# Two prompt tiles and the samples as a dense pass over all experts; gathered V rows split 14 to 2

## The chip, the cores and the metric

One core of a Trainium2 chip. The time is that of one launch on the device, in microseconds; lower is better. Data is float32 throughout.

## What is computed

One decoder layer over 1024 prompt tokens and 64 sample tokens (8 sequences of 8), width 1024: a token mix (dilated window attention in three groups and a short gated convolution), then experts, then a last norm. The change is in the experts:

```python
def block(xb):                                   # per token, 8 heads
    q = (xb @ w_query).reshape(PEER_BLOCK, PEER_HEADS, 2, half)
    s1 = einsum('thd,kd->thk', q[:, :, 0], sub_keys[0]); s2 = ... q[:, :, 1], sub_keys[1]
    v1, i1 = top_k(s1, 16); v2, i2 = top_k(s2, 16)
    cand = v1[..., :, None] + v2[..., None, :]   # 256 sums
    top_s, top_pos = top_k(cand, 16)             # 16 of 128*128 experts
    gate = softmax(top_s)
    act = einsum('td,thkd->thk', xb, expert_u[eidx])
    return einsum('thk,thkd->td', gate * gelu(act), expert_v[eidx])
x = x + gate2 * out;  y = rmsnorm(x, norm_f_g)
```

`expert_u` and `expert_v` have 16384 rows of 1024 numbers (64 MB each). A token takes 128 rows of each.

## The kernel before, in words

Tokens lie in nine tiles of 128: 0 to 7 prompt, tile 8 (`PS`) the 64 samples. They go in four segments (`SEG_TILES`: tile 0; 1, 2; 3 to 5; 6, 7 and the samples). Two programs run beside each other on every engine.

The **background** is the token mix of a segment and then its queries: `chain_order` writes out the order of all uses of four PSUM banks (`psB`), keyed as `("qkv", g, z)`, `("conv", ...)`, `("s", ...)` (attention scores), `("mix", ...)`, `("out", ...)`, and at the end of a segment per tile and head `project`, `turn_q`, `score`. Every use is filled by TensorE and emptied by ScalarE (ACT) or VectorE (DVE); a bank can be filled again only when its use four places back is emptied. Weights come through three slots of `w`, loaded by SyncE (SP) in `weight_blocks` order. Each score (128 tokens x 256 numbers) is copied to memory by ACT.

The **jobs** are the experts: one job per tile and head, 72 in all (`JOBS`). For job s, DVE ranks the scores (`experts`, L1960 to L2022: 16 best of each half, 16 best of 256 sums, their numbers, the gates), GpSimd (POOL) gathers row k of `expert_u` for all 128 tokens by an indirect DMA into a ring (`gather_u`, L863) and of `expert_v` one job later (`gather_v`, L873), one row of each in turn. DVE forms the dot of each U row (`dot`, L2033, one fused instruction) and at the end of the job the coefficients (`coefs`, ends in L2073; waits once for ACT). The V rows are added up in two ways (`on_vector`): on DVE by multiply-add into `acc` (`add_row`, L2049), or on TensorE (`weigh`, L1251) by a matmul with a diagonal matrix that ACT writes (L1649) into the accumulators `psA`. Before, 8 of 16 rows went to either in the first 56 jobs and 5 to DVE, 11 to TensorE after. The sample tile has 64 tokens, so its 16 rows are gathered as 8 (`width`), two halves that TensorE folds at the end. After 8 jobs a tile is summed, gated, normed and stored (`gather_up`, `final`, `finish`).

What ties the two together is `limit(s, f)`: at fraction f of job s each engine runs its background up to the same key. The key is found by planned costs (`chain_cost`, a unit about 1 us of matmul) spread evenly between marks, and every engine meets the keys in its own fixed order:

```python
marks = [(0, lead)]
marks += [(HEADS * T0[g] - 3, number["score", item_of(HEADS * T0[g])]) for g in range(1, SEGS_N)]
marks += [(HEADS * T0[SEGS_N - 1] + 3, last_bg)]
```

So before, the marks are at jobs 0, 5, 21, 45 and 51, and by these costs a job has 62, 33, 28 and 16 units of background in turn; jobs 51 to 72 have none.

## Time and profile before

| | us |
|---|---|
| median of 3 runs | 4099.45 (4091.34 to 4104.18) |
| the profiled execution | 4089.54 |
| its span, first to last instruction | 4087.7 |
| TensorE busy (PE) | 3203.6, 78% |
| VectorE busy (DVE) | 2904.9, 71% |
| GpSimd busy (POOL) | 2238.6, 55% |
| ScalarE busy (ACT) | 671.2, 16% |
| mean granted TensorE clock | 0.875 of full |

"Busy" is the time with an instruction of that engine running, its waits left out. A float32 matmul shows as two halves, so counts of PE are twice those of the code; a transpose shows as one. The DMA share is the mean over 16 DMA engines and can pass 1.0, since packets overlap.

### The profile page before, as it was taken

To read this page: it belongs to the slowest core of one execution; us is meant where nothing else is said; L and a number is where in the kernel's file an instruction comes from. 1 tells how busy PE (TensorE), PEld (TensorE's weight loads), DVE (VectorE), ACT (ScalarE), POOL (GpSimd) and SP (SyncE) were. 2 spreads that over 40 slices of the span, in tenths; PEclk is the share of its full clock that TensorE was granted. 3 is DMA by queue.
4 is the path that set the end of the run, shared out by engine and by line. 5 is a ranking of instruction groups with operands and counts; after the bars stand their busy time and mean duration, and the time that the engine had idled before them with its cause. 6 is when DMAs were issued, how large, how long until landed. Compare 5 with 4: busy or idle time off the path is not lost.

```text
span 4087.7 us, 35782 instructions
## 1 busy us (share of the span) xinstructions
PE 3203.6 (78%) x10406; PEld 1817.5 (44%) x10406; DVE 2904.9 (71%) x6586; ACT 671.2 (16%) x1872; POOL 2238.6 (55%) x2189
## 2 busy tenths in 40 slices
PE   5987989888889998887888977677877765566566
PEld 2575757654445544554444543334544431122222
DVE  1215645678876687677887777767778888888887
ACT  0012021221012211222101331111111110010111
POOL 0003323555554566565665566545657677777765
PEclk8988979999997899998998888788988877788878
DMA  6989969999997899999999899999999999999998
GB/s 207 274 268 334 316 219 315 368 404 383 389 364 244 289 385 398 377 394 382 391 394 366 307 359 366 359 365 363 400 355 406 407 407 409 409 399 409 409 368 319
DMA packets 670924, 1458.83 MB, mean 357 GB/s; under 512 B 53745, under 2 KB 378737, under 8 KB 670705
## 3 DMA queue, kind: packets, MB, share of 16 engines
q0 software_dynamic: 313648, 1142.49, 72.4%
q1 hardware_dynamic: 316596, 267.84, 21.0%
q10 hardware_dynamic: 40488, 46.22, 3.3%
q8 instruction: 87, 1.43, 0.1%
q14 instruction: 105, 0.86, 0.1%
HBM read 1422.53 MB, written 33.83 MB: 356 GB/s over the span
## 4 chain that ended last, share of the span: by engine, by line
DMA 17%; DVE 9%; POOL 9%; PE 8%; issue 5%; SPq 3%; ACT 1%; ACTq 0%; DVEq 0%; POOLq 0%
DMA peer_vring<-in_expert_v,peer_idx 12%; POOL peer_uring L863 4%; POOL peer_vring L873 4%; PE peer_psA L1251 4%; DVE peer_uring L2033 3%; DMA peer_uring<-in_expert_u,peer_idx 2%; DVE peer_acc L2049 2%; SPq L715 2%; SPq L711 1%; DMA peer_w<-in_w_in 1%; DMA peer_w<-in_w_attn_o 1%; PE peer_psB L1075 1%; PE peer_psB L1098 1%; PE peer_psB L1143 1%; DMA peer_arena<-in_x_prompt 1%
## 5 line engine op out<-in xcount | busy, mean ns | idle before, releaser
L1251 PE MATMUL peer_psA<-peer_vring,peer_diag 128*128 128x512 f32 x2336 | 1321.4, 704 | 527.2 <-DMA peer_vring<-in_expert_v,peer_idx 345.9
L873 POOL DMA_INDIRECT peer_vring<-in_expert_v,peer_idx x1088 | 1115.9, 1026 | 1129.2 <-PE peer_psA L1251 837.1
L2033 DVE CUSTOM_DVE_ANT_0 peer_uring<-peer_uring,peer_psH 128x1024 f32<-128x1024 f32 x1088 | 1320.8, 1214 | 327.3 <-DMA peer_uring<-in_expert_u,peer_idx 322.5
L863 POOL DMA_INDIRECT peer_uring<-in_expert_u,peer_idx x1088 | 1117.0, 1027 | 498.9 <-issue 299.2
L1251 PEld LDWEIGHTS peer_psA<-peer_vring,peer_diag 128*128 128x128 f32 x2336 | 485.6, 222 | 1184.5 <-issue 999.5
L2049 DVE SCALAR_TENSOR_TENSOR peer_acc<-peer_vring,peer_coef,peer_acc 128x1024 f32<-128x1024 f32 x495 | 637.1, 1287 | 89.8 <-DMA peer_vring<-in_expert_v,peer_idx 84.3
L1143 PE MATMUL peer_psB<-peer_hT,peer_w 128*128 128x128 f32 (+3 forms) x1152 | 277.0, 399 | 32.7 <-DMA peer_w<-in_w_in 32.5
L1220 PE MATMUL peer_psB<-peer_w,peer_hT 128*128 128x256 f32 x1152 | 275.8, 395 | 30.0 <-DMA peer_w<-in_w_query 29.3
L1036 PE MATMUL peer_psB<-peer_w,peer_hT 128*128 128x384 f32 (+1 forms) x864 | 294.9, 496 | 1.4 <-issue 0.7
L1164 PE MATMUL peer_psB<-peer_hT,peer_w 128*128 128x128 f32 (+3 forms) x1024 | 257.8, 407 | 35.0 <-DMA peer_w<-in_w_attn_o 35.0
L1220 PEld LDWEIGHTS peer_psB<-peer_w,peer_hT 128*128 128x128 f32 x1152 | 229.2, 201 | 89.3 <-DMA peer_w<-in_w_query 31.5
L1143 PEld LDWEIGHTS peer_psB<-peer_hT,peer_w 128*128 128x128 f32 x1152 | 199.2, 193 | 116.7 <-DMA peer_w<-in_w_in 36.3
L1164 PEld LDWEIGHTS peer_psB<-peer_hT,peer_w 128*128 128x128 f32 x1024 | 182.7, 198 | 111.6 <-DMA peer_w<-in_w_attn_o 39.5
L1036 PEld LDWEIGHTS peer_psB<-peer_w,peer_hT 128*128 128x128 f32 (+1 forms) x864 | 161.8, 190 | 131.3 <-issue 44.1
L1698 ACT ACTIVATE peer_g<-peer_g 128x16 f32<-128x16 f32 (+1 forms) x72 | 15.5, 215 | 1139.5 <-DVE peer_g L2063 1138.0
L1649 ACT ACTIVATE peer_diag<-peer_ident,peer_coef 128x128 f32<-128x128 f32 x584 | 178.3, 387 | 54.9 <-DVE peer_coef L2073 54.9
L1832 DVE TENSOR_REDUCE peer_mx<-peer_psB 128x1 f32<-128x512 f32 (+2 forms) x92 | 56.1, 626 | 124.0 <-PE peer_psB L1075 123.4
L1193 PE MATMUL peer_psB<-peer_w,peer_mT 128*128 128x384 f32 (+3 forms) x432 | 130.3, 458 | 6.3 <-issue 4.5
L1075 PE MATMUL peer_psB<-peer_w,peer_mT 64*128 64x256 f32 (+3 forms) x272 | 121.6, 532 | 0.0
L1098 PE MATMUL peer_psB<-peer_w,peer_arena 128*128 128x64 f32 x648 | 102.0, 317 | 24.2 <-ACT peer_arena L1511 24.0
L1098 PEld LDWEIGHTS peer_psB<-peer_w,peer_arena 128*128 128x128 f32 x648 | 99.1, 235 | 35.9 <-issue 35.9
L1193 PEld LDWEIGHTS peer_psB<-peer_w,peer_mT 128*128 128x128 f32 (+1 forms) x432 | 80.8, 188 | 59.0 <-issue 19.7
(201 smaller groups left out, 2738.0 us busy)
## 6 DMA issues: line engine op xcount, KB each, us to landing
peer_w<-in_w_in SPq DMA_DIRECT2D x136, 512.0 KB, 9.0
peer_w<-in_w_in SPq DMA_DIRECT2D x24, 1536.0 KB, 17.1
peer_w<-in_w_query SPq DMA_DIRECT2D x32, 1024.0 KB, 17.0
peer_w<-in_w_ada SPq DMA_DIRECT2D x16, 1536.0 KB, 8.0
peer_uring<-in_expert_u,peer_idx POOLq DMA_INDIRECT x1088, 11.4
peer_vring<-in_expert_v,peer_idx POOLq DMA_INDIRECT x1088, 11.2
peer_w<-in_w_conv_o SPq DMA_DIRECT2D x32, 384.0 KB, 10.0
peer_w<-in_w_o SPq DMA_DIRECT2D x8, 1536.0 KB, 22.2
```

The lines of the kernel that those rows point to most:

```text
L863: pool.indirect_dma_start(out=uring[:, r % U, :], out_offset=None, in_=io["expert_u"], in_offset=bass.IndirectOffsetOnAxis(ap=idx[:, s % 4 ...
L873: pool.indirect_dma_start(out=vring[:, r % V, :], out_offset=None, in_=io["expert_v"], in_offset=bass.IndirectOffsetOnAxis(ap=idx[:, s % 4 ...
L1036: last = pe.matmul(dst[0:R, 0:WQKV], hT[:, k, i * P:i * P + R], wv[:, k, :], start=(k == 0), stop=(k == DC - 1))
L1098: last = pe.matmul(bank(key_o)[:, 0:HD], pT[:, t_slot[g, it, b] % 2, (at % 4) * P:(at % 4 + 1) * P], vv[:, kb, col:col + HD], start=(at == ...
L1143: last = pe.matmul(dst[:, 0:m], wv[:, k, part, :], hT[:, k, 0:m], start=(k == 0), stop=(k == DC - 1))
L1164: last = pe.matmul(dst[:, 0:m], wv[:, KC_AT[q] + k, :], src[:, k, 0:m], start=(k == 0), stop=(k == KC[q] - 1))
L1193: last = pe.matmul(dst[0:R, 0:e - a], mT[:, k, i * P:i * P + R], wv[:, k, :], start=(k == 0), stop=(k == DC - 1))
L1220: last = pe.matmul(dst[:, 0:KD], hT[:, k, j * P:(j + 1) * P], wv[:, k, :], start=(k == 0), stop=(k == DC - 1))
L1251: last = pe.matmul(psA[:, c * 512:(c + 1) * 512], diag[:, a % DG, :], vring[:, r % V, c * 512:(c + 1) * 512], start=first, stop=False, ski ...
L1649: act.activation(diag[:, a % DG, :], ident[:], ACT.Copy, scale=coef[:, s % 4, k:k + 1]).then_inc(diag_set, 1)
L2033: dve.tensor_tensor_reduce(uring[:, r % U, :], uring[:, r % U, :], psH[:], 1.0, 0.0, ALU.mult, ALU.add, act_[:, k:k + 1]).then_inc(u_used, 1)
L2049: dve.scalar_tensor_tensor(out=acc[:], in0=vring[:, r % V, :], scalar=c, in1=acc[:], op0=ALU.mult, op1=ALU.add).then_inc(v_added, 1)
```

## The change

- Jobs are only those of tiles 0 to 5 (`TD = 6`, 48 jobs). In them `on_vector` gives 14 of 16 V rows to DVE, all but k = 5 and 11. The U ring has 8 rows, not 9. The half-wide jobs go.
- A table in memory has a number for each of 16384 experts and each of the 320 tokens of tiles 6, 7 and samples (21 MB). POOL zeroes it by 8 DMAs, one after each of jobs 0 to 7.
- The 24 scores of segment 3 are not stored. DVE ranks each straight from its bank, as part of the background (`rank`), ACT forms its exponentials (`raise_gates`), and POOL adds the 16 gates per token to the table by 16 indirect DMAs (`scatter`), each of one number per partition. A scatter waits for the one of the previous head of its tile.
- Behind the last score the background has the dense pass (`dense_order`), 128 blocks of 128 experts: SP loads the block of U and the table's rows, and of V three blocks later; TensorE turns U (`ut`, 8 transposes), forms all dots for 320 tokens (`at`, 8 matmuls of 320 columns); ACT squares, DVE and ACT form the gelu, DVE multiplies by the table's gates; TensorE multiplies by V (`vd`, for four blocks at a time, three tiles and two halves), and DVE adds that to sums in memory on the chip. SP reads the table only when all scatters have landed, and asks for the second block of U behind that.
- The marks of `limit` are at jobs 0, 5, 21 and 48. By the planned costs jobs 21 to 48 have 92 units each.
- At the end the three tiles are gated, normed and stored.

```diff
 PS = SEQ // P
 SEG_TILES = ((0,), (1, 2), (3, 4, 5), (6, 7, 8))
+TD = 6
...
-JOBS = NT * HEADS
-WINDOW = 56
+JOBS = TD * HEADS
+ND = NT - TD
+DENSE_AT = tuple(d * P for d in range(ND))
+TDN = (ND - 1) * P + NS
+N_EXP = KEYS * KEYS
+CHUNKS = N_EXP // P
+GROUP = 4
+V_LAG = 6
...
 def on_vector(s, k):
-    return k in ((1, 3, 5, 7, 9, 11, 13, 15) if s < WINDOW else (2, 5, 8, 11, 14))
+    return k not in (5, 11)
...
+def dense_order():
+
+    order = [("ht", d, c) for d in range(ND) for c in range(2)]
+    for c in range(CHUNKS + V_LAG):
+        if c < CHUNKS:
+            order += [("ut", c, half) for half in range(2)]
+        group, d = divmod(c - V_LAG, GROUP)
+        if group >= 0 and d < ND:
+            order += [("vd", group, d, half) for half in range(2)]
+        if 1 <= c <= CHUNKS:
+            order += [("at", c - 1)]
+    return order
...
-        marks += [(HEADS * T0[g] - 3, number["score", item_of(HEADS * T0[g])]) for g in range(1, SEGS_N)]
-        marks += [(HEADS * T0[SEGS_N - 1] + 3, last_bg)]
+        marks += [(HEADS * T0[g] - 3, number["score", item_of(HEADS * T0[g])]) for g in range(1, SEGS_N) if T0[g] < TD]
+        marks += [(JOBS, last_bg)]
...
+            def scatter(n):
+                t, it = dense_items[n]
+                g, R = place(t)[0], rows_of(t)
+                yield min(number["score", it] + 24, number["ht", 0, 0])
+                if n == 0:
+                    pool.wait_ge(zeroed, 16 * 8)
+                old = n - sum(t2 >= TD for t2 in SEG_TILES[g])
+                if old >= dense_before(g):
+                    pool.wait_ge(scattered[old % 4], 16 * TOPK * (old // 4 + 1))
+                pool.wait_ge(d_ready, n + 1)
+                for k in range(TOPK):
+                    pool.indirect_dma_start(
+                        out=io["table"], out_offset=bass.IndirectOffsetOnAxis(ap=d_idx[0:R, n % 4, k:k + 1], axis=0),
+                        in_=d_gate[0:R, n % 4, k:k + 1], in_offset=None, compute_op=ALU.add).then_inc(scattered[n % 4], 16)
...
+            for c in range(CHUNKS + 3):
+                if c < CHUNKS:
+                    if c >= 3:
+                        wait_filled(sp, ("ut", c - 3, 1))
+                    elif c:
+                        sp.wait_ge(zeroed, 16 * 8)
+                    sp.dma_start(u_slot[c % 3], io["expert_u"][c * P:(c + 1) * P, :]).then_inc(eu_in[c % 3], 16)
+                    if c == 0:
+                        for r in range(4):
+                            sp.wait_ge(scattered[r], 16 * TOPK * (len(dense_items) // 4))
+                        for r in range(2):
+                            wait_emptied(sp, ("st", 4 * r + 3))
+                    if c >= 4:
+                        sp.wait_ge(ct_set, c - 3)
+                    sp.dma_start(g_slot[c % 4], table[c * P:(c + 1) * P, :]).then_inc(g_in[c % 4], 16)
...
+                    elif key[0] == "at":
+                        for k in range(DC):
+                            last = pe.matmul(dst[:, 0:TDN], UT[:, c % 2, k * P:(k + 1) * P], HT[:, k, :],
+                                             start=(k == 0), stop=(k == DC - 1))
+                    else:
+                        group, d, half = key[1:]
...
+                            last = pe.matmul(dst[0:R, :], COEF[:, c % (2 * GROUP), at:at + R],
+                                             v_slot[c % (2 * GROUP)][:, 512 * half:512 * (half + 1)],
+                                             start=(c % GROUP == 0), stop=(c % GROUP == GROUP - 1))
...
+                    dve.scalar_tensor_tensor(out=t2, in0=t2, scalar=1.0, in1=a, op0=ALU.add, op1=ALU.mult).then_inc(a_inner, 1)
+                    dve.wait_ge(g_in[c % 4], 16 * (c // 4 + 1))
+                    dve.tensor_tensor(g2, a, g2, ALU.mult).then_inc(out_of(key), 1)
...
+                dve.tensor_tensor(a, a, g_slot[c % 4], ALU.mult).then_inc(ct_set, 1)
```

The order on POOL in jobs 28 and 29, where before only U and V gathers took turns. L954 and L964 are the gathers of U and V, L979 the scatters; the sixteen of one head are one row.

```order
L954 DMA peer_uring<-in_expert_u,peer_idx 128x1024
L964 DMA peer_vring<-in_expert_v,peer_idx 128x1024
L979 DMA gates_of_experts<-peer_d_gate,peer_d_idx 5242880x1 x16
L954 DMA peer_uring<-in_expert_u,peer_idx 128x1024
L964 DMA peer_vring<-in_expert_v,peer_idx 128x1024
L979 DMA gates_of_experts<-peer_d_gate,peer_d_idx 5242880x1 x16
L954 DMA peer_uring<-in_expert_u,peer_idx 128x1024
L964 DMA peer_vring<-in_expert_v,peer_idx 128x1024
```

So from U row 12 of job 28 on, 16 or 32 scatters stand behind each pair of gathers, for eleven pairs; the last 160 stand in one piece behind row 7 of job 29.

The order on DVE in the same jobs, where before a ranking was cut into 15 pieces over a job's 16 rows. L2353 is the dot, L2369 the addition, L1983 to L2034 a ranking of the new kind (this is its start).

```order
L2353 ISA peer_uring,peer_act<-peer_uring,peer_psH 128x1024
L2353 ISA peer_act 128x1
L2369 SCALAR_TENSOR_TENSOR peer_acc<-peer_vring,peer_coef,peer_acc 128x1024
L1983 MAX peer_mT<-peer_psB 128x8 x2
L1986 MAX_INDEX peer_d_i<-peer_mT,peer_psB 128x8
L1987 MATCH_REPLACE peer_mT<-peer_mT,peer_psB 128x128
L1986 MAX_INDEX peer_d_i<-peer_mT,peer_psB 128x8
```

24 whole rankings stand from row 6 of job 28 to row 7 of job 29, one or two behind each row. TensorE in the dense pass reads as below; L1070 is `at`, L1060 `ut`, L1078 `vd`, L1410 a weighed row.

```order
L1070 MATMUL peer_psB<-peer_arena,peer_mT 128x320 x8
L1060 MATMUL peer_psB<-peer_ident,peer_w 128x128 x8
L1078 MATMUL peer_psB<-peer_w,peer_arena 128x512 x4
L1410 MATMUL peer_psA<-peer_vring,peer_diag 128x512 x2
L1078 MATMUL peer_psB<-peer_w,peer_arena 128x512 x4
L1070 MATMUL peer_psB<-peer_arena,peer_mT 128x320 x8
L1060 MATMUL peer_psB<-peer_ident,peer_more 128x128 x8
```

Two weighed rows stand in some seven blocks of this, where before 8 or 11 stood in each job.

## Rows read from the trace of the kernel before

**Rows 1.** The page: all packets, and those of the plain queue.
```profile
DMA packets 670924, 1458.83 MB, mean 357 GB/s; under 512 B 53745, under 2 KB 378737, under 8 KB 670705
...
q1 hardware_dynamic: 316596, 267.84, 21.0%
```

**Rows 2.** Table of stretches: PE, PEld, DVE, ACT, POOL busy, clock, DMA share, GB/s.
```profile
400.00:820.00 420.00, 384.32 (x1509) 276.14 (x1508) 240.76 (x561) 79.55 (x214) 162.26 (x162) 0.92 0.88 307
820.00:1150.00 330.00, 288.53 (x885) 162.87 (x884) 263.89 (x581) 47.57 (x127) 192.22 (x188) 0.93 1.04 390
1150.00:1420.00 270.00, 240.84 (x850) 137.74 (x849) 186.99 (x434) 71.59 (x206) 131.59 (x130) 0.82 0.80 288
1420.00:1700.00 280.00, 246.17 (x722) 139.61 (x721) 216.69 (x459) 47.91 (x105) 166.06 (x160) 0.95 1.03 385
1700.00:3240.00 1540.00, 1200.11 (x3964) 686.87 (x3962) 1175.77 (x2597) 278.28 (x793) 938.20 (x901) 0.87 1.01 374
...
3290.00:3910.00 620.00, 372.53 (x621) 135.40 (x619) 524.36 (x1186) 58.29 (x198) 467.51 (x467) 0.81 1.02 404
```

**Rows 3.** The same stretches for L2073 alone, one instruction per job, on DVE.
```profile
400.00:820.00 420.00, 1.04 (x6) 0.92 0.88 307
...
1700.00:3240.00 1540.00, 4.90 (x28) 0.87 1.01 374
...
3290.00:3910.00 620.00, 2.62 (x15) 0.81 1.02 404
3910.00:4087.00 177.00, 1.16 (x7) 0.83 0.90 346
```

**Rows 4.** The same table for L1251 alone, the weighed rows on PE.
```profile
1700.00:3240.00 1540.00, 500.95 (x894) 184.11 (x892) 0.87 1.01 374
```

**Rows 5.** The groups by line: weighed rows, dots, additions.
```profile
L1251 PE MATMUL peer_psA<-peer_vring,peer_diag 128*128 128x512 f32 x2336 | 1321.4, 704 | 527.2 <-DMA peer_vring<-in_expert_v,peer_idx 345.9
...
L2033 DVE CUSTOM_DVE_ANT_0 peer_uring<-peer_uring,peer_psH 128x1024 f32<-128x1024 f32 x1088 | 1320.8, 1214 | 327.3 <-DMA peer_uring<-in_expert_u,peer_idx 322.5
...
L2049 DVE SCALAR_TENSOR_TENSOR peer_acc<-peer_vring,peer_coef,peer_acc 128x1024 f32<-128x1024 f32 x495 | 637.1, 1287 | 89.8 <-DMA peer_vring<-in_expert_v,peer_idx 84.3
```

**Rows 6.** Timeline of PE: start, duration (us); x counts halves or transposes.
```profile
405.06 0.49 PE L1047 MATMUL peer_psB<-peer_ident,peer_arena 128*128 128x128 f32 x3
405.39 1.88 PE L1251 MATMUL peer_psA<-peer_vring,peer_diag 128*128 128x512 f32 x4
...
1018.53 5.32 PE L1036 MATMUL peer_psB<-peer_w,peer_hT 128*128 128x384 f32 x16
1023.69 3.60 PE L1251 MATMUL peer_psA<-peer_vring,peer_diag 128*128 128x512 f32 x8
1027.13 5.32 PE L1036 MATMUL peer_psB<-peer_w,peer_hT 128*128 128x384 f32 x16
```

**Rows 7.** The table for PE alone: busy, clock, DMA share, GB/s.
```profile
1000.00:1060.00 60.00, 59.79 (x173) 1.00 1.01 374
...
1200.00:1300.00 100.00, 86.06 (x322) 0.73 0.71 257
```

**Rows 8.** Groups by line and form: DVE and ACT reading PSUM.
```profile
L1511 ACT ACTIVATE peer_arena<-peer_psB 128x512 f32<-128x512 f32 x68 | 38.6, 590 | 56.2 <-PE peer_psB L1111 55.6
...
L1769 DVE TENSOR_TENSOR peer_arena<-peer_psB,peer_arena 128x512 f32<-128x512 f32 x16 | 11.0, 689 | 7.1 <-PE peer_psB L960 6.9
...
L1769 DVE TENSOR_TENSOR peer_arena<-peer_psB,peer_arena 128x320 f32<-128x320 f32 x8 | 3.9, 485 | 0.0
```

**Rows 9.** Groups by line: three of the instructions of a ranking.
```profile
L1993 DVE TENSOR_TENSOR peer_eq<-peer_ab,peer_iota 128x512 f32<-128x512 uint32 x72 | 49.7, 690 | 0.2
...
L1963 DVE FIND_INDEX8 peer_i<-peer_v,peer_sc 128x8 uint32<-128x128 f32 x144 | 41.4, 288 | 0.0
...
L1974 DVE MAX8 peer_best<-peer_eq 128x8 f32<-128x256 f32 x72 | 30.4, 422 | 0.5
```

**Rows 10.** The timeline of POOL in the pure gathering stretch.
```profile
3521.32 0.94 POOL L873 DMA_INDIRECT peer_vring<-in_expert_v,peer_idx  x1 [0.30 <-issue]
```

More of the change, by code:

```diff
@@ L123, in constants @@
         "rope": rope, "pmask": pmask, "smask": smask, "ident": np.eye(P, dtype=np.float32),
+        "columns": np.array([[DENSE_AT[d] + min(p, rows_of(TD + d) - 1) for d in range(ND)] for p in range(P)], np.float32),
         "iota": np.tile(np.arange(TOPK, dtype=np.float32), (P, 1)),
@@ L270, in added_by @@
     for s in range(JOBS):
-        for k in range(width(s)):
+        for k in range(TOPK):
             mine = on_dve if on_vector(s, k) else on_pe
@@ L875, in gather_v, with background @@
                     in_offset=bass.IndirectOffsetOnAxis(ap=idx[:, s % 4, k:k + 1], axis=0)).then_inc(v_in[r % V], 16)
+            def scatter(n):
[8 more added lines that the diff above has]
+                pool.wait_ge(d_ready, n + 1)
+                for k in range(TOPK):
+                    pool.indirect_dma_start(
+                        out=io["table"], out_offset=bass.IndirectOffsetOnAxis(ap=d_idx[0:R, n % 4, k:k + 1], axis=0),
+                        in_=d_gate[0:R, n % 4, k:k + 1], in_offset=None, compute_op=ALU.add).then_inc(scattered[n % 4], 16)
+            def background():
+                for n in range(len(dense_items)):
+                    yield from scatter(n)
+            pace = Pace(background())
+            wide = io["table"].rearrange("(p q m) o -> p q (m o)", p=P, m=512)
+            pool.memset(zero, 0.0).then_inc(zero_set, 1)
+            pool.wait_ge(zero_set, 1)
             for s in range(JOBS + 1):
@@ L1272, in _ @@
                     weigh(r)
-                    pace.up_to(limit(s, min(0.9, (i + 3) / len(rows))))
-            pe.wait_ge(summed, NT)
-            for c in range(2):
-                for i in range(2):
-                    last = pe.matmul(psA[0:NS, c * 512:(c + 1) * 512], ident[:, i * NS:(i + 1) * NS],
-                                     acc[:, c * 512:(c + 1) * 512], start=(i == 0), stop=(i == 1))
-            last.then_inc(folded, 1)
+                    pace.up_to(limit(s, min(0.9, (r % TOPK + 6) / TOPK)))
         @block.scalar
@@ L1600, in keep_queries @@
                         act.dma_start(io["scores"][(T0[g] + j) * HEADS + h],
-                                      sc_out[:, it % 2, :]).then_inc(sc_stored[it % 2], 16)
+                                      sc_out[:, q % 2, :]).then_inc(sc_stored[q % 2], 16)
+                    if i >= 3 and first + i - 3 in dense_no:
+                        yield from raise_gates(first + i - 3)
+                if first + count - 1 in dense_no:
+                    yield from raise_gates(first + count - 1)
@@ L1642, in spread @@
                 act.wait_ge(coef_set, s + 1)
-                for k in range(width(s)):
+                for k in range(TOPK):
                     r = rows_before(s) + k
@@ L1738, in background @@
                     yield from shift_tile(g, size(g) - 1)
+                    first, count = T0[g] * HEADS, size(g) * HEADS
+                    norms = {norm_at(g + 1, i): i for i in range(size(g + 1))} if g + 1 < SEGS_N else {}
+                    for i in range(count):
+                        if first + i in dense_no:
+                            yield from rank(first + i, dense_before(g))
+                        if i in norms:
+                            yield from norm_shift(g + 1, norms[i])
@@ new lines, in background, with raised @@
+                    if first + count - 1 in dense_no:
+                        yield number["score", first + count - 1]
+                        raised(dense_no[first + count - 1])
+                yield from weigh_all()
+            def raised(q):
+                dve.wait_ge(d_exp, q + 1)
+                if q:
+                    dve.wait_ge(d_ready, q)
+                link(dve.reciprocal(d_rg, d_dg[:, q % 2:q % 2 + 1]))
+                link.wait()
+                dve.tensor_scalar(d_gate[:, q % 4, :], d_eg[:, q % 2, :], d_rg, None, ALU.mult).then_inc(d_ready, 1)
@@ L2137, in _ @@
                     gather_up(t - 1)
-            finish(NT - 1)
+            finish(TD - 1)
+            dve.wait_ge(gate_s_in, 16)
+            for d in range(ND):
+                R = rows_of(TD + d)
+                for half in range(2):
+                    wait_emptied(dve, ("vd", CHUNKS // GROUP - 1, d, half))
+                gate_d = gate_s if TD + d == PS else gate2
+                dve.tensor_tensor(sums[d][0:R, :], sums[d][0:R, :], gate_d[0:R, :], ALU.mult).then_inc(d_gated, 1)
+                dve.wait_ge(d_gated, d + 1)
+                dve.wait_ge(xd_in[d], 16)
+                dve.tensor_tensor(xd[d][0:R, :], sums[d][0:R, :], xd[d][0:R, :], ALU.add).then_inc(d_x2, 1)
+            for d in range(ND):
+                R = rows_of(TD + d)
+                dve.wait_ge(d_rooted, d + 1)
+                link(dve.reciprocal(fin[0:R, 2, d:d + 1], fin[0:R, 1, d:d + 1]))
+                link.wait()
+                dve.scalar_tensor_tensor(out=xd[d][0:R, :], in0=xd[d][0:R, :], scalar=fin[0:R, 2, d:d + 1],
+                                         in1=gainf[0:R, :], op0=ALU.mult, op1=ALU.mult).then_inc(d_y, 1)
 def layer(nc, io):
```

359 lines of the change are left out of this document (287 added, 72 removed).

## The prediction

> **What bounds the kernel now.** I read the page first, then a table of stretches, then single lines. The page's totals [rows 1] say that 1459 MB move at a mean of 357 GB/s. The table of stretches [rows 2] says where that is the limit: from 820 to 1150, 1420 to 1700 and 3290 to 3910 us the DMA share is above 1.0, while TensorE (PE) and VectorE (DVE) have slack; 1700 to 3240 stands at 1.01. Two stretches are different. In 400 to 820 and 1150 to 1420 the share is 0.88 and 0.80 and PE is busy for 91% and 89% (384.32 of 420, 240.84 of 270): the dense layers and the attention of a segment set the pace there. The last step of a job's coefficients is one instruction per job, so its count [rows 3] dates the jobs: 6 end in 400 to 820, 28 in 1700 to 3240, 15 in 3290 to 3910, 7 after that; with one more in the 50 us between, 15 are left for 820 to 1700, and job 21 starts near 1700. A job of pure gathering costs 620/15 = 41.3 us: 32 rows of 512 KB (16.8 MB) at 404 GB/s. **So the last 850 us are bound by bytes, and the change removes bytes.** The question is what stands in their place.
>
> **What it takes off.** 24 jobs go, 8 of them half wide: 320 of 1088 rows of U and as many of V, 336 MB, 830 us at 404 GB/s. PE loses 488 of 584 weighed rows: four halves of a matmul each at 0.43 us (a run of 8 takes 3.44 us from start to start [rows 6]), 1.72 us a row, 840 us of work at full clock. DVE loses 320 dots at 1.21 us and gains 672 - 504 = 168 additions at 1.29 us [rows 5]: 388 us less, 216 more.
>
> **What it adds.** U and V once (134 MB), the table written and read (42 MB), 384 scatters of one number per partition, 24 rankings on DVE that were there before, and the dense pass. By the order that the program has now, this does not lie evenly: the background between jobs 21 and 48 is dealt out by planned cost, 92 units a job where it was 28. I cut the run into five parts.
>
> **A, up to job 21 (1700 us before).** The background is the same, jobs have 14 additions on DVE and 2 on PE. A pure job keeps DVE busy for 524.36/15 = 35.0 us; with 9 more additions 46.5 us. In the byte-bound stretches (11 jobs, 610 us) DVE was busy for 44 us of 55 a job; with 6 more additions it is at 52. That fits, with less to hide a late row in: +30 us. In the two other stretches (10 jobs) 6 rows of PE go (10.3 us a job) and 7.7 us of DVE come; these phases alternate between the engines, so I take them as -10 us together, between -90 (all PE's gain) and +60. Zeroing moves 21 MB, 52 us of transfers in jobs 0 to 7, half beside idle queues: +25. A = 1745, between 1640 and 1800.
>
> **B, job 21 to the first dense ranking (7.4 jobs).** PE without weighed rows was busy 1200.11 - 500.95 = 699 us in 1700 to 3240 [rows 2, 4] and 21 us in the 50 us after: 720 us for the rest of segment 2 and all of segment 3, spread over 30 jobs under the gathers. Of it the last 24 queries (16 halves of 256 columns and little else, 4.5 us each, 109 us) belong to C. 611 us and 15 rows at 1.72 are 637 us, now in 7.4 jobs. The nearest rows are the two stretches with PE at 91% and 89%, which would give 700 to 715; with 14 additions DVE answers attention later, so I take 740, between 650 (98% busy) and 850 (75%).
>
> **C, rankings and scatters (1.1 jobs).** 24 rankings follow each other on DVE. One is three passes over 512 numbers, ten instructions over 128, six over 256 [rows 9], and some 16 small ones of 0.1 to 0.2 us: 2.05 + 2.85 + 2.5 + 2.0 = 9.4 us, 226 us for all; before they were spread over 24 jobs. With 1.1 jobs of row work (51) DVE needs 277 us. POOL needs more: an indirect DMA takes it 0.94 us and 0.30 before it, 1.25 us [rows 10]. 16 items of 128 rows are 320 us, 8 items of 64 rows between 80 and 160 (I take 100), and 22 gathers between them 28. The first scatter waits for two rankings (25 us), and behind the last SyncE reads the table, which the first block needs (some 17 us with both landings). 490 us; PE has 110 us of work in it, and no dot can run ahead of the gathers behind the scatters. Below: 300, if an issue of 4-byte elements takes half as long and DVE sets the end. Above: no row shows a transfer that adds in memory. 40,960 elements, read and written, at the 43 ns that a packet of the plain queue cost (21.0% of 16 engines' 4088 us over 316596 packets [rows 1]) are 220 us on 16 engines, hidden; if an issue costs double because memory is both read and written, the part is 910. The Trainium skill (DMA: Bandwidth & Descriptors, "Anatomy of one DMA") fits a software-issued DMA at about 2.0 us plus its bytes; if these 512-byte scatters went singly at that, an estimate from that page, the sum would be some 290 us higher. The row stands among gathers whose transfers overlap, so the sum keeps 1.25.
>
> **D, the dense pass (18.5 jobs, 128 blocks).** Per block PE does 8 transposes at 0.11 us (three in 0.33), 16 halves of 320 columns at 5.16/16 x 320/384 = 0.269 us, and a quarter of 48 halves of 512 columns at 0.43 [rows 6]: 0.88 + 4.30 + 5.16 = 10.34 us, 1323 us in all, and 37 weighed rows make 1387. DVE: 18.5 x 46.5 = 860 us and per block three passes of 320 and 1.5 of 512 at 0.485 and 0.689 [rows 8], 319 us: 1179, and some 0.6 us per block of waiting for ScalarE's square, 1256. ScalarE: two copies of 512 at 0.59 [rows 8] and two shorter passes, about 2 us a block, hidden. Bytes: 310 + 134 + 21 MB at 404 GB/s, 1151 us, hidden. PE sets the end with DVE close behind and four PSUM banks between them, and ScalarE stands still at each job's end until the coefficients are out. I take PE at 88%, 1580 us, between 1420 (98%) and 1850 (75%).
>
> **E, the end**: last sums, three tiles of gate, norm and store: 25 us.
>
> **Sum**: 1745 + 740 + 490 + 1580 + 25 = 4580 us of span against 4087.7; 2 us lie around it, and the median of the runs is 10 us above the profiled one, so 4590. PE has replaced the transfers as the limit, and C is a hole in which nearly everything stands.
>
> **Rivals.**
> *Tight packing, 4150 (slower side or even).* A 1690, B 650, C 350, D 1430, E 25. For it: PE at 99.7% for 60 us at full clock [rows 7] with gathers beside it. Against: C needs cheap scatters.
> *Bytes stay the limit, 3920 (the other side).* -830 for gathers, +332 for U and V, +110 for the table and small loads, +220 for the scattered elements is about -170 against 4088. It decides if C hides behind gathers and PE never falls under 95%; PE's total, 3204 - 488 x 2.26 [rows 5] + 1323 = 3424 us, allows it, the order of C speaks against.
> *Half clock in the dense pass, 4850.* The granted clock was 1.00 where PE was 99.7% busy and 0.73 (a mix of 2.4 and 1.2 GHz) where it was 86% busy with short gaps [rows 7]. Gaps at every hand-over with DVE would stretch D from 1580 to some 1850. The Trainium skill (TensorE: Matmul & The Clock Gate, Part 1) has it that activity releases the throttle and idleness brings it back; by that rule it feeds itself.
> *Scatters dearer than gathers, 5000 and more.* C at 910 or above; no row speaks for it, none against.
>
> **Numbers.** Forecast 0.60, tight packing 0.14, bytes 0.07, half clock 0.13, slow scatters 0.06. All bounds at one end would give 4035 or 5435; taken as independent (root of the squares of 105, 90, 190, 160 below and 55, 110, 420, 270 above) they give 4306 and 5094, and the upper ends of C and D are rivals of their own, so the forecast alone stands for 4300 to 4850. The range goes to 4180 and 4900, for most of the tight case and of the half clock. 0.3% is about what a measurement of this kernel can tell from no change: faster 0.07, same 0.02, slower 0.91.
>
> **What would show it.** DMA share under 0.8 in the second half; PE idle and clock low in one stretch of 350 to 550 us near 2500, with POOL's scatters end to end and DVE on rankings first, then idle; jobs of 80 to 90 us in the dense pass with PE near 88%; jobs of about 100 us between 1745 and 2500. A dense pass with jobs under 77 us, or scatters issued in under 0.7 us, proves parts D or C wrong; gathers at 400 GB/s after 1745 would prove the whole reading wrong.

## The result, and the profile after

The changed kernel takes 4933.44 us (median of 4 runs, 4930.31 to 4947.73) against 4097.19 us for the kernel before on the same chip: 1.2047 times as long, 95% interval 1.2016 to 1.2078. The forecast was 4590 in a range up to 4900: the direction came out, the size did not. The profiled execution spans 4931.9 us (4087.7 before).

The page first: all packets and the two data queues, which answer to [rows 1], and the slices of PE and of the bandwidth.

```profile
PE   6978886567787699986785203105999999899995
...
PEclk9989798788668899858897656557999999999998
DMA  7899899999789998739973322227988989889984
...
DMA packets 679528, 1293.21 MB, mean 262 GB/s; under 512 B 96241, under 2 KB 431473, under 8 KB 679281
...
q0 software_dynamic: 273840, 828.06, 48.7%
q1 hardware_dynamic: 372324, 424.10, 26.6%
```

The bytes went down by 166 MB and the mean rate from 357 to 262 GB/s: after 1755 us, as the table below shows, transfers no longer set the pace. In PE's row there is a hole of some six slices (of 123 us each), in which the DMA digit is 2 or 3, and then an almost solid row of nines.

The table of stretches of the changed kernel, cut at the bounds of the parts A to E (PE, PEld, DVE, ACT, POOL busy, granted clock, DMA share, GB/s). It answers to [rows 2].

```profile
400.00:1755.00 1355.00, 1013.32 (x3458) 663.96 (x3466) 1037.55 (x2144) 207.98 (x520) 729.86 (x648) 0.80 0.95 344
1755.00:2600.00 845.00, 729.78 (x2766) 470.98 (x2773) 449.08 (x935) 163.34 (x455) 275.22 (x234) 0.84 0.79 256
2600.00:3375.00 775.00, 151.98 (x571) 122.16 (x571) 253.15 (x944) 32.49 (x114) 616.01 (x414) 0.59 0.28 30
3375.00:4890.00 1515.00, 1428.43 (x4752) 794.03 (x4752) 1102.93 (x2166) 308.94 (x653) 745.27 (x601) 0.98 0.87 314
4890.00:4932.00 42.00, 1.72 (x3) 0.25 (x1) 20.92 (x21) 7.06 (x13) 0.00 (x0) 0.54 0.30 100
```

And the same stretches for L2393, the last step of a job's coefficients, one instruction per job on DVE, as in [rows 3]:

```profile
400.00:1755.00 1355.00, 3.67 (x21) 0.80 0.95 344
1755.00:2600.00 845.00, 1.22 (x7) 0.84 0.79 256
2600.00:3375.00 775.00, 0.17 (x1) 0.59 0.28 30
3375.00:4890.00 1515.00, 3.31 (x19) 0.98 0.87 314
```

The jobs lie as the prediction put them: 21, then 7, one, and 19. The cuts are rounded: the first ranking starts at 2611.9 us and the first transpose of the dense pass at 3374.1, so by the events themselves B is some 12 us longer and C as much shorter. Set beside its sum:

| part | predicted (range) | measured | difference |
|---|---|---|---|
| A, to job 21 | 1745 (1640 to 1800) | 1755 | +10 |
| B, to the first dense ranking | 740 (650 to 850) | 845 | +105 |
| C, rankings and scatters | 490 (300 to 910) | 775 | +285 |
| D, dense pass | 1580 (1420 to 1850) | 1515 | -65 |
| E, end | 25 | 42 | +17 |
| span | 4580 | 4932 | +352 |

Each part is inside its own bounds, but two of them missed upwards together. The most is in C, where POOL is busy for 616 of 775 us, DVE for 253 and PE for 152. Below are the shares of the chain that ended last, the page's group of the scatters, and the instruction of a ranking in which DVE waits for them:

```profile
PE peer_psB L1078 14%; POOL gates_of_experts L979 11%; PE peer_psB L1070 10%; PE peer_psB L1323 3%; PE peer_psA L1410 3%; PE peer_psB L1302 2%; PE peer_psB L1234 2%; PE peer_psB L1257 2%; PE peer_psB L1060 2%; PE peer_psB L1195 2%; DVE peer_acc L2369 2%; DMA peer_vring<-in_expert_v,peer_idx 1%; DVE peer_uring L2353 1%; PE peer_psB L1379 1%; PE peer_psB L1352 1%
...
L979 POOL DMA_INDIRECT gates_of_experts<-peer_d_gate,peer_d_idx x384 | 587.2, 1529 | 176.8 <-issue 116.0
...
L2034 DVE TENSOR_SCALAR peer_d_idx<-peer_mT,peer_columns 128x16 uint32<-128x16 f32 x24 | 6.2, 260 | 333.8 <-DMA gates_of_experts<-peer_d_gate,peer_d_idx 333.5
```

POOL's timeline in the hole (start, duration in us, idle time before it in brackets). The last row is a scatter of 64 rows, of the sample tile; the others work on 128:

```profile
2757.96 1.56 POOL L979 DMA_INDIRECT gates_of_experts<-peer_d_gate,peer_d_idx  x1 [0.30 <-issue]
2759.82 0.99 POOL L954 DMA_INDIRECT peer_uring<-in_expert_u,peer_idx  x1 [0.30 <-issue]
2761.12 0.97 POOL L964 DMA_INDIRECT peer_vring<-in_expert_v,peer_idx  x1 [0.30 <-issue]
2762.40 1.61 POOL L979 DMA_INDIRECT gates_of_experts<-peer_d_gate,peer_d_idx  x1 [0.30 <-issue]
...
2794.32 1.41 POOL L979 DMA_INDIRECT gates_of_experts<-peer_d_gate,peer_d_idx  x1 [0.30 <-issue]
```

A gather is issued in 0.97 to 0.99 us (0.94 in [rows 10]). A scatter that adds takes 1.56 us, and hardly less with half the rows. It moves 512 bytes where a gather moves 512 KB. The detail of the scatters' line (duration in ns, first and last start, forms; then the time from issue to landing):

```profile
L979 POOL DMA_INDIRECT gates_of_experts<-peer_d_gate,peer_d_idx x384: 1404/1556/2408, 2633.2 to 3364.0; - x192
...
DMA to landing us min/median/max: 2.7/3.0/8.5
```

384 scatters are 587.2 us of POOL and 116.0 us between them, 703 us of the 733 from first to last. DVE stood still for 333.5 us in the rankings, because the scatters of the ranking four places back had not all landed and its indices could not yet be overwritten. A scatter has landed 3.0 us after its issue and the DMA share is 0.28, which speaks against a queue in the transfers; the runs below test it.

### The profile page after: what moved, and what is told of

Same layout as the page of the kernel before. It is cut to its first block, busy times and chain, and to the rows that moved or that the text cites. A ratio compares the mean times of both kernels' runs of the same rounds, so it can differ in the third digit from the quotient of the medians.

```text
span 4931.9 us, 42120 instructions
## 1 busy us (share of the span) xinstructions
PE 3644.5 (74%) x13062; PEld 2260.1 (46%) x13078; DVE 2970.1 (60%) x6503; ACT 769.5 (16%) x1870; POOL 2403.9 (49%) x1942
## 4 chain that ended last, share of the span: by engine, by line
PE 46%; POOL 13%; DVE 6%; DMA 5%; issue 5%; ACT 2%; SPq 1%; ACTq 0%; DVEq 0%; POOLq 0%
PE peer_psB L1078 14%; POOL gates_of_experts L979 11%; PE peer_psB L1070 10%; PE peer_psB L1323 3%; PE peer_psA L1410 3%; PE peer_psB L1302 2%; PE peer_psB L1234 2%; PE peer_psB L1257 2%; PE peer_psB L1060 2%; PE peer_psB L1195 2%; DVE peer_acc L2369 2%; DMA peer_vring<-in_expert_v,peer_idx 1%; DVE peer_uring L2353 1%; PE peer_psB L1379 1%; PE peer_psB L1352 1%
## 5 line engine op out<-in xcount | busy, mean ns | idle before, releaser
L954 POOL DMA_INDIRECT peer_uring<-in_expert_u,peer_idx x768 | 1037.1, 1350 | 1635.4 <-DVE peer_act L2353 1370.1
L2353 DVE CUSTOM_DVE_ANT_0 peer_uring<-peer_uring,peer_psH 128x1024 f32<-128x1024 f32 x768 | 925.5, 1207 | 119.2 <-DMA peer_uring<-in_expert_u,peer_idx 117.6
L964 POOL DMA_INDIRECT peer_vring<-in_expert_v,peer_idx x768 | 765.2, 996 | 471.2 <-issue 229.9
L2369 DVE SCALAR_TENSOR_TENSOR peer_acc<-peer_vring,peer_coef,peer_acc 128x1024 f32<-128x1024 f32 x666 | 851.6, 1279 | 8.1 <-DMA peer_vring<-in_expert_v,peer_idx 6.7
L1078 PE MATMUL peer_psB<-peer_w,peer_arena 128*128 128x512 f32 (+1 forms) x1536 | 692.1, 603 | 58.5 <-issue 57.7
L979 POOL DMA_INDIRECT gates_of_experts<-peer_d_gate,peer_d_idx x384 | 587.2, 1529 | 176.8 <-issue 116.0
L1070 PE MATMUL peer_psB<-peer_arena,peer_mT 128*128 128x320 f32 x2048 | 578.4, 436 | 0.0
L1070 PEld LDWEIGHTS peer_psB<-peer_arena,peer_mT 128*128 128x128 f32 x2048 | 386.9, 191 | 199.7 <-issue 58.7
L1078 PEld LDWEIGHTS peer_psB<-peer_w,peer_arena 128*128 128x128 f32 (+1 forms) x1536 | 261.6, 175 | 428.4 <-issue 425.0
L1410 PE MATMUL peer_psA<-peer_vring,peer_diag 128*128 128x512 f32 x384 | 225.9, 719 | 298.8 <-DMA peer_vring<-in_expert_v,peer_idx 235.3
L1410 PEld LDWEIGHTS peer_psA<-peer_vring,peer_diag 128*128 128x128 f32 x384 | 80.6, 225 | 385.8 <-issue 343.9
L2034 DVE TENSOR_SCALAR peer_d_idx<-peer_mT,peer_columns 128x16 uint32<-128x16 f32 x24 | 6.2, 260 | 333.8 <-DMA gates_of_experts<-peer_d_gate,peer_d_idx 333.5
```

What stands on the lines that cost most here:

```text
L954: pool.indirect_dma_start(out=uring[:, r % U, :], out_offset=None, in_=io["expert_u"], in_offset=bass.IndirectOffsetOnAxis(ap=idx[:, s % 4 ...
L964: pool.indirect_dma_start(out=vring[:, r % V, :], out_offset=None, in_=io["expert_v"], in_offset=bass.IndirectOffsetOnAxis(ap=idx[:, s % 4 ...
L979: pool.indirect_dma_start(out=io["table"], out_offset=bass.IndirectOffsetOnAxis(ap=d_idx[0:R, n % 4, k:k + 1], axis=0), in_=d_gate[0:R, n ...
L1070: last = pe.matmul(dst[:, 0:TDN], UT[:, c % 2, k * P:(k + 1) * P], HT[:, k, :], start=(k == 0), stop=(k == DC - 1))
L1078: last = pe.matmul(dst[0:R, :], COEF[:, c % (2 * GROUP), at:at + R], v_slot[c % (2 * GROUP)][:, 512 * half:512 * (half + 1)], start=(c % G ...
L1410: last = pe.matmul(psA[:, c * 512:(c + 1) * 512], diag[:, a % DG, :], vring[:, r % V, c * 512:(c + 1) * 512], start=first, stop=False, ski ...
```

## Experiments

Each run stands beside its own runs of the kernel before (medians 4097 to 4099 us). Ratios are against that kernel, with their 95% intervals. Differences from the changed kernel are differences of medians, and good to some 20 us, since two intervals of about 0.3% enter. The length of the dense pass is taken from the first to the last `at` product (3375.9 to 4852.0 us in the change, 1476 us).

Three theories were open. The hole C: is it the adding scatter's issue on POOL, the transfers of the adding, or the rankings on DVE? The dense pass D: is PE its limit? And is it the dense pass or the new split of V rows that costs in the rest?

### Scatters that write instead of adding

```diff
-                        in_=d_gate[0:R, n % 4, k:k + 1], in_offset=None, compute_op=ALU.add).then_inc(scattered[n % 4], 16)
+                        in_=d_gate[0:R, n % 4, k:k + 1], in_offset=None).then_inc(scattered[n % 4], 16)
```

An expert that is chosen twice by one token keeps only the last gate here; all instructions stay.

> The 384 scatters write their number instead of adding it to the table; all else as in the change, so an expert that two heads of a token choose keeps one gate (that part of the sum is left out). Theory 1 (POOL's own time to issue an indirect DMA to memory sets the ranking stretch, and adding is not what makes it dear): step of 1.86 us from scatter to scatter stays within 0.1 us, time within 40 us of 4933. Theory 2 (the add is the price: 0.57 us more than a gather's 1.29 us step): step falls to 1.3 us, 384 x 0.55 = 210 us less, some 4720. Theory 3 (memory latency of a read and a write sets it): landing falls from 3.0 us, step with it.

4728.95 us, ratio 1.1539 (1.1505 to 1.1573), 204 us less than the change. The scatters' detail and two of them in POOL's timeline:

```profile
L979 POOL DMA_INDIRECT gates_of_experts<-peer_d_gate,peer_d_idx x384: 896/972/2022, 2638.8 to 3159.7; - x192
...
  DVE peer_d_idx L2034: 167.0, 17
...
DMA to landing us min/median/max: 2.0/2.1/6.5
```

```profile
2679.70 0.97 POOL L979 DMA_INDIRECT gates_of_experts<-peer_d_gate,peer_d_idx  x1 [0.31 <-issue]
...
2688.86 0.90 POOL L979 DMA_INDIRECT gates_of_experts<-peer_d_gate,peer_d_idx  x1 [0.30 <-issue]
```

Without the addition the median falls from 1556 to 972 ns, which is a gather's price, and the time from the first scatter's start to the last one's from 731 to 521 us. That is the whole gain, and it is what theory 2 forecast (4720). The landing fell from 3.0 to 2.1 us as well, as theory 3 had it, but issues go on while transfers are under way, and 384 times 0.58 us of issue (224 us) explains the 210 us. So the price is paid in POOL's time for the issue. What POOL does in the added 0.58 us no view shows.

### One scatter of sixteen

```diff
-                for k in range(TOPK):
+                for k in range(1):
                     pool.indirect_dma_start(
```

(and 16 instead of 16 * TOPK in the three waits on them). 15 of 16 gates never enter the table.

> Only the first of each head's 16 scatters is issued; 15 of 16 gates are left out of the table. Theory 1 (scatters on POOL set the stretch between the first ranking and the dense pass, 2600 to 3370 us): it shrinks to what DVE needs, 24 x 9.4 + 51 = 277 us and some handing over, 300 us; total 4933 - 460 = 4470. Rival (DVE's 24 rankings in a row set it): stretch shrinks by under 100 us, total over 4830.

4455.01 us, ratio 1.0867 (1.0836 to 1.0899): 478 us less, as forecast (4470). The table of the hole and of the dense pass behind it, the scatters' detail, and two scatters in POOL's timeline of this run:

```profile
2630.00:2890.00 260.00, 129.67 (x468) 103.25 (x468) 238.00 (x900) 26.64 (x98) 63.32 (x50) 0.74 0.26 72
2890.00:4400.00 1510.00, 1427.25 (x4746) 793.25 (x4747) 1092.52 (x2157) 308.82 (x653) 741.09 (x598) 0.98 0.86 315
...
L979 POOL DMA_INDIRECT gates_of_experts<-peer_d_gate,peer_d_idx x24: 1409/1566/1619, 2639.2 to 2884.0; - x24
...
2751.38 1.61 POOL L979 DMA_INDIRECT gates_of_experts<-peer_d_gate,peer_d_idx  x1 [7.65 <-DVE peer_d_gate L1973]
...
2764.92 1.48 POOL L979 DMA_INDIRECT gates_of_experts<-peer_d_gate,peer_d_idx  x1 [8.96 <-DVE peer_d_gate L1973]
```

DVE is now busy for 238 of 260 us: the rankings set the end of C, which lasts 276 us from the start of the first of them (2617.9) to the first dense dots (2893.6). The prediction's 277 for DVE alone was right. The dense pass is as long as in the change, 1482 against 1476 us: what came in C did not come back later. The run also settles whether a scatter is dear because it queues behind earlier ones. Here nearly every scatter stands alone, with POOL idle for some 5 to 12 us before it, and the median is still 1566 ns. The added time belongs to each issue.

### Half of the first dense product

```diff
-                        for k in range(DC):
+                        for k in range(DC // 2):
                             last = pe.matmul(dst[:, 0:TDN], UT[:, c % 2, k * P:(k + 1) * P], HT[:, k, :],
-                                             start=(k == 0), stop=(k == DC - 1))
+                                             start=(k == 0), stop=(k == DC // 2 - 1))
```

The tokens' product with U is summed over half the width only, with four matmuls instead of eight.

> The dots of the dense pass are formed over half the width (4 of 8 matmuls a block; wrong dots, half of that product left out). Theory 1 (TensorE sets the end of the dense pass): 128 x 2.15 us = 275 us less PE work; DVE needs 18.5 x 46.5 + 128 x 3.1 = 1256 us against 1112 us of PE, so the pass falls from 1520 us to some 1310, total 4720. Rival (DVE or the hand-over of PSUM banks sets it): under 60 us less.

4790.73 us, ratio 1.1685 (1.165 to 1.1719): 143 us less. 4 matmuls, or 8 halves, fewer in each of 128 blocks are 1024 x 0.269 = 275 us of PE work. The dense pass (3381.2 to 4709.2) became 148 us shorter, and its table reads:

```profile
3420.00:4650.00 1230.00, 1084.64 (x3403) 554.00 (x3402) 994.25 (x1991) 279.53 (x592) 677.93 (x542) 0.95 0.94 354
```

In the same stretch the change has PE at 95%, DVE at 74% and a DMA share of 0.88. Here PE fell to 88%, DVE rose to 81% and the share to 0.94. PE is the first limit of D, but only about half of what is taken from it comes out; behind it DVE and the transfers stand close, and no run shows which of the two takes over. The 213 us that were expected were too much.

### V rows split 8 to 8 in all jobs

```diff
-    return k not in (5, 11)
+    return k % 2 == 1
```

> V rows split 8 to 8 in all 48 jobs, the rest as in the change. PE gets 6 x 1.72 = 10.3 us a job, DVE loses 7.7. In the dense pass (18.5 jobs) PE sets the end: +190 us. In jobs 0 to 21, where DVE had become the limit (1755 us instead of 1700): -40 us. In 21 to 28.4 PE +76 us. Ranking stretch unchanged. Total 5150. Rival (the 14 additions on DVE are what slows the run): total under 4900.

5103.09 us, ratio 1.2443 (1.2404 to 1.2483): 170 us more than the change. Job 21 ends at 1745 us, where it ended at 1753: up to there the split is worth 8 us, not the 40 that were expected. The first ranking starts 35 us later, so some 40 us are lost in part B. The dense pass takes 1609 us instead of 1476:

```profile
3420.00:4650.00 1230.00, 1199.85 (x3911) 653.40 (x3911) 739.23 (x1591) 262.71 (x585) 463.83 (x448) 1.00 0.80 292
```

PE stands at 98%, DVE at 60%. Six more rows a job in 18.5 jobs are 191 us of PE, of which 133 show. Within the change the 14 to 2 split is thus right, mostly because the dense pass needs PE.

### The kernel before with the 14 to 2 split alone

```diff
-    return k in ((1, 3, 5, 7, 9, 11, 13, 15) if s < WINDOW else (2, 5, 8, 11, 14))
+    return k not in (5, 11)
...
-                first = r == rows_before(t * HEADS)
+                first = a == weighed_before(t * HEADS)
```

(The second edit only tells the accumulating matmul where a tile's first weighed row is.)

> The kernel before with the V rows split 14 to 2 in all jobs and nothing else. Theory (DVE takes the bound from the transfers: a pure job needs 46.5 us of DVE and about 1.5 us of waiting for ScalarE): jobs 51 to 64 take 48 us instead of 41.3, jobs 0 to 21 end at 1755 instead of 1700 as in the change, jobs 21 to 51 gain little; total 4097 + 55 + 30 x 2 + 20 x 6.5 = 4340. Rival (PE's relief repays it, by fewer waits for V rows): within 60 us of 4097.

4317.61 us, ratio 1.0524 (1.0505 to 1.0542). The table in its pure gathering stretch:

```profile
3500.00:4000.00 500.00, 81.58 (x88) 25.83 (x88) 491.02 (x995) 18.25 (x62) 392.14 (x355) 0.54 1.00 380
```

DVE is busy for 98%, and 11 jobs end in 500 us, about 45 us each, where 41.3 were enough for the bytes. DVE's 491.02 us are 44.6 us a job, 2 us under the 46.5 of the prediction's part A. The DMA share still reads 1.00 here, at 380 GB/s instead of 404. The split by itself costs 220 us, as forecast (4340).

### Background spread over more jobs

```diff
-        marks += [(HEADS * T0[g] - 3, number["score", item_of(HEADS * T0[g])]) for g in range(1, SEGS_N) if T0[g] < TD]
+        marks += [(26, number["ht", 0, 0])]
```

The due points at jobs 5 and 21 go, and one at job 26 for the start of the dense pass's own work takes their place. Nothing is left out.

> The marks of the background at jobs 5 and 21 go; one mark puts the start of the dense pass at job 26 and 22 instead of 29.5 jobs' worth... in plain words: all background before the dense pass is dealt evenly over jobs 0 to 26 (63 planned units a job), the dense pass over jobs 26 to 48 (76 units a job). Theory (each stretch is set by its busiest engine, so even dealing uses TensorE in jobs 7 to 21, where it was 60 to 78% busy, and takes load off 21 to 28): up to the rankings 400 + 26 x 68 = 2170 us instead of 2600, rankings and scatters 760 as before, dense pass 22 jobs with DVE (46.5 + 5.8 x 3.1 = 64.5 us) and PE (63.4) near each other, 70 us a job = 1540; total 4350 to 4500. Rival (transfers or the chain of hand-overs bound the first half anyway): total over 4750.

4804.06 us, ratio 1.1726 (1.1707 to 1.1746): 129 us less than the change, but 300 more than was expected. The tables of the first half, of an attention stretch in it, of the hole and of the dense pass:

```profile
400.00:2430.00 2030.00, 1727.88 (x6301) 1136.75 (x6300) 1321.95 (x2771) 360.14 (x957) 881.01 (x763) 0.84 0.89 306
1100.00:1300.00 200.00, 178.16 (x581) 114.75 (x582) 95.40 (x213) 50.31 (x142) 52.66 (x45) 0.54 0.45 148
2440.00:3210.00 770.00, 130.84 (x438) 102.76 (x437) 266.45 (x929) 28.13 (x99) 635.04 (x431) 0.58 0.31 39
3216.00:4716.00 1500.00, 1418.06 (x4723) 788.26 (x4720) 1215.47 (x2423) 318.87 (x672) 844.87 (x686) 0.98 0.94 348
```

The first ranking starts at 2422.6 us, 189 us earlier than in the change. The expectation had it at 2170. That is where it missed: the 23 jobs that end between 404 and 2357 us took 85 us each instead of 68, although no engine was full there (PE 85%, DVE 65%, DMA share 0.89). The rival that was written down beside it, that the transfers or the chain of hand-overs bound the first half, had put the total over 4750, and the total is there. Which of the two it is stays open; in the attention the clock was 0.54. The hole stayed as long as expected and a little longer, 794 us from the first ranking to the first dense dots against 764 in the change, with POOL busy for 635 of 770 us. The dense pass has 22 jobs in it now and is 1497 us long, with DVE at 81% and a DMA share of 0.94.

### Both: spread background, one scatter of sixteen

The two diffs above together; 15 of 16 gates never enter the table.

> As the one before last with only 1 of 16 scatters per head (15 of 16 gates left out): what the dense pass would cost with scatters nearly free. Theory: the same as that kernel less 460 us, 3900 to 4050. Rival: if the scatters' time was hidden by more even jobs, under 300 us less.

4321.63 us, ratio 1.0552 (1.0531 to 1.0573). Against the spread background alone it is 482 us less, which repeats the 478 of the same edit on the change; 460 were expected. The absolute expectation (3900 to 4050) missed, because it was built on the one before. Even with nearly free scatters and this order, the kernel with the dense pass and the new split is 5.5% slower than the one before: its dense stretch of 1498 us has PE at 95% (1418.13 us busy).

### More matmuls in the attention

The granted clock in the attention of part B was low. The table of the attention of segment 3 in the changed kernel, and PE's groups that are the same instructions in both kernels, first before (L1075, L1098 and L1111, between 2190 and 2560 us), then in the changed kernel (2030 to 2260):

```profile
2060.00:2200.00 140.00, 121.14 (x357) 73.81 (x362) 45.55 (x103) 32.01 (x89) 22.35 (x19) 0.50 0.30 93
```

```profile
L1075 PE MATMUL peer_psB<-peer_w,peer_mT 64*128 64x512 f32 (+3 forms) x80 | 36.5, 536 | 0.0
L1098 PE MATMUL peer_psB<-peer_w,peer_arena 128*128 128x64 f32 x232 | 30.7, 282 | 3.6 <-ACT peer_arena L1511 3.5
L1111 PE MATMUL peer_psB<-peer_ident,peer_arena 128*128 128x128 f32 x116 | 21.0, 315 | 7.3 <-ACT peer_arena L1492 7.1
```

```profile
L1234 PE MATMUL peer_psB<-peer_w,peer_mT 64*128 64x512 f32 (+3 forms) x80 | 60.6, 856 | 2.3 <-issue 2.1
L1257 PE MATMUL peer_psB<-peer_w,peer_arena 128*128 128x64 f32 x232 | 47.7, 383 | 3.7 <-ACT peer_arena L1667 3.6
L1270 PE MATMUL peer_psB<-peer_ident,peer_arena 128*128 128x128 f32 x116 | 27.8, 396 | 8.2 <-ACT peer_arena L1648 8.1
```

A granted clock of 0.50 is the 1.2 GHz level for all of 140 us, although PE is busy for 87% of it. These three groups take 136.1 us instead of 88.2, 48 us more for the same counts. Two runs test whether more work on PE lifts the clock, by repeating the mask matmuls of the attention (the extra results are thrown away), one on the change and one on the kernel before:

```diff
+                            for _ in range(3):
+                                pe.matmul(to, identb[:], mask[:, m0 * P:(m0 + run) * P], start=True, stop=True)
                             pe.matmul(to, identb[:], mask[:, m0 * P:(m0 + run) * P], start=True, stop=False)
```

> The change, and in the attention each matmul that writes the mask into a bank is done four times over (the first three are overwritten): 0.64 us more of TensorE per bank at 2.4 GHz, 1.3 us at 1.2 GHz, and nothing else; it puts steady wide matmuls among the small ones, where TensorE ran at 1.2 GHz (granted 0.50) from 2060 to 2200 us. Theory 1 (it is the kind and steadiness of TensorE's work there that lets the clock fall, and the fall costs some 50 to 70 us in segment 3 and as much in segment 2): the granted clock in that stretch rises to over 0.8, and the run is 0 to 80 us shorter in spite of the added work. Theory 2 (the clock does not follow from such work, or the chain through ScalarE and DVE sets the stretch): clock near 0.50 as before and the run 32 banks x 1.3 + 40 more, 50 to 90 us, longer.

4998.6 us, ratio 1.2201 (1.2173 to 1.2229): 65 us more, as theory 2 had it (50 to 90).

> The same repetition of the mask matmuls in the kernel before, where the attention of segment 2 stood at a granted clock of 0.82 and that of segment 3 is covered by transfers. Theory 1: clock up, 0 to 30 us less (4070 to 4097). Theory 2: the added work shows, 4097 to 4140.

4158.74 us, ratio 1.0138 (1.0118 to 1.0158): 60 us more, a little above what theory 2 had (up to 4140). The extra work costs its own time in both kernels and wins nothing. The attention of segment 3, each from its first score matmul to its last, in the change and in the change with more masks (PE alone: busy, clock, DMA share, GB/s):

```profile
2047.00:2198.00 151.00, 129.91 (x377) 0.53 0.35 111
```

```profile
2092.00:2261.00 169.00, 151.82 (x502) 0.59 0.32 99
```

The clock rose from 0.53 to 0.59 and no further. The split has more to do with it. The same table for the attention of segment 2, first the kernel before, then the change, the change with 8 to 8, and the kernel before with 14 to 2; the last is the attention of segment 3 in the kernel before:

```profile
1181.00:1375.00 194.00, 167.38 (x598) 0.78 0.75 270
```

```profile
1235.00:1436.00 201.00, 164.91 (x525) 0.61 0.73 256
```

```profile
1227.00:1417.00 190.00, 164.28 (x589) 0.79 0.77 277
```

```profile
1229.00:1455.00 226.00, 180.71 (x537) 0.57 0.64 223
```

```profile
2214.00:2353.00 139.00, 119.08 (x452) 0.86 0.91 322
```

With 21 weighed rows beside this attention the clock is 0.78 and 0.79, with 5 or 6 of them 0.61 and 0.57, in both kernels. In segment 3 it is 0.86 in the kernel before (18 weighed rows) and 0.53 in the change (one). The split also takes additions from DVE, so these runs don't show that the weighed rows alone do it. What exactly makes the clock fall stays open. It is not the busy share of PE alone: in segment 3 that is 86% in both kernels.

## Why the prediction was right or wrong

**What bounds the kernel: right.** The gathers' last 850 us went, and no stretch of the table after 1755 us is above 314 GB/s. PE replaced the transfers outside the hole.

**A: right in size, in part by luck.** 1755 for 1745. The forecast gave the split +20 of its 45 us and the zeroing of the table 25. The 8 to 8 run ends job 21 at 1745 us against 1753 in the change and 1693 in the kernel before, so the split is worth 8 us here and the other 52 come with the rest of the change. No run parts the zeroing from the remaining edits. In the kernel before the split alone ends job 21 at 1783. Why the change is 30 us better off with the same split was not traced.

**B: mis-sized, +105.** The set of instructions was as forecast, and 611 + 26 us of PE were the terms for it. PE was busy for 729.78 us, 698 of them without the 15 weighed rows, which took only 31.76. The term that failed is the durations: they came from before, where this work ran under weighed rows at a clock of 0.87 over the stretch, and in the attention it now ran at 0.50 to 0.53, where the kernel before had 0.86 (0.73 beside 86% busy had stood in [rows 7]). The three groups above hold 48 of the 87 us by which the work without weighed rows grew; the other 39 were not traced. PE stood still for 115 of 845 us and was busy for 86%, just the share that the forecast had taken (637 of 740). The prediction had a rival for half clock, but put it in the dense pass, which ran at 0.98.

**C: the step that failed.** "16 items of 128 rows are 320 us, 8 items of 64 rows between 80 and 160 (I take 100)" priced a scatter like a gather, and half the rows at less than a whole issue. A scatter of 128 rows measured 1.56 us and 0.30 before it instead of 0.94 and 0.30, one of 64 rows 1.41 and 0.30: 703 us for 384 instead of 420. That is 283 of the 285 us by which C was long; the 72 us around it were forecast as 70. The plain write parts the 283: without the addition the 384 issues take 494 us (376.9 busy, 116.8 between them), so the addition is 209 us of it, and the remaining 74 are mostly the guess for 64 rows, which cost 0.90 and 0.30 even without it. The one-of-sixteen run shows that DVE's 277 us are the floor under it.

The upper bound (an issue costs double, C at 910) had the mechanism, and the issue with its gap is 1.5 times that of a plain one. The choice of the lower value was the error: the row taken did not add in memory, as the prediction itself said. That the bytes of the addition are hidden was right, with a DMA share of 0.28. The Trainium skill (DMA: Bandwidth & Descriptors, "Anatomy of one DMA") fits a DMA issued by software at about 2.0 us plus its bytes. An estimate from this figure of the Trainium skill is 384 x 2.0 = 768 us for the scatters and 838 for C. The prediction's "some 290 us higher" (C at 780) took the difference to 1.25 us for all 384, though its sum held only 100 us for the 128 scatters of 64 rows. Both are nearer to the 775 measured than the forecast, but the plain write follows at 1.2 to 1.3 us with the same 512 bytes, so the figure is not the pace of issues. It is near the landing time of a plain scatter, 2.1 us.

**D: right,** 1515 for 1580. PE was busy for 1428 us in it (1387 forecast), and at 94% instead of 88%: the work was mis-sized by 41 us one way and the waits by more the other. One block's matmuls in PE's timeline of the changed kernel:

```profile
4011.37 1.04 PE L1060 MATMUL peer_psB<-peer_ident,peer_w 128*128 128x128 f32 x8
4012.25 4.47 PE L1070 MATMUL peer_psB<-peer_arena,peer_mT 128*128 128x320 f32 x16
...
4020.81 8.80 PE L1078 MATMUL peer_psB<-peer_w,peer_arena 128*128 128x512 f32 x16 [3.22 <-issue]
```

From start to start the eight transposes take 0.88 us and the sixteen halves 4.31, as forecast (0.88 and 4.30). Before the next product with V PE stands still for 3.22 us. Gaps of this kind make up the remaining 6%; the view names no releaser for this one, so that it is a hand-over with DVE is not shown.

**E:** 42 for 25, the last sums and stores; it was not looked into.

**The rivals.** Tight packing and the transfers as limit are out (C and the DMA share). Half clock came, but in B and not in D. Scatters dearer than gathers had 0.06 and is the nearest to what happened, at two thirds of its price. The range to 4900 ended 33 us short because its upper end was set by the half clock in D alone. The prediction's own spread of all parts together reached 5094, and C alone at its bound would have given 5010: cutting the range below both left out the case that came. Outside C the misses partly cancel: 105 more in B and 65 less in D.

## What to carry to other kernels

Price a stream of small indirect DMAs by the issue on its engine, not by its bytes: 384 scatters of at most 512 bytes each held the kernel for 700 us, and each that adds in memory cost half as much again as one that only writes. Before work is moved from transfers to an engine, add up that engine where the work is to go: here PE was at 78% in 1700 to 3240 us and got 1323 us of new work for 830 us of transfers saved, and rankings that had been spread over 24 jobs run in series once they must all be done before the dense pass. A retuning that is right for the new limit (14 to 2, worth 170 us in the change) can be wrong for the old one (220 us lost in the kernel before), so the two are measured apart.

## What the runs showed of the hardware

- The addition in memory is paid at the issue: a median of 1556 ns against 972 on POOL for the same 128 elements, and 1566 ns where each scatter stands alone. Half the rows save 0.15 us with the addition (1.41 for 1.56) and 0.07 without it (0.90 for 0.97).
- A granted clock of 0.50 held for 140 us with PE busy for 87% and never still for more than 1.93 us. More mask matmuls in that attention raised it from 0.53 to 0.59 only. With the 8 to 8 split in place of 14 to 2, and so 21 weighed rows beside the attention of segment 2 instead of 5 or 6, it was 0.78 instead of 0.57 in the kernel before, and 0.79 instead of 0.61 in the change.
- In the dense pass, with PE at 94% to 98% busy, the mean clock was 0.98 to 1.00; with PE at 88% it was 0.95.
